# A two-layer backbone in split fp32: seven products in place of eight for 18 of the 22 gate/up blocks of the first feed-forward

## The reference, cut to what matters

```python
D_MODEL, SEQ, CTX_LEN = 1024, 512, 256
FFN_HIDDEN = -(-8 * D_MODEL // (3 * 256)) * 256    # 2816
def swiglu(h, w_in, w_out):
    gate, up = jnp.split(h @ w_in, 2, axis=-1)
    return (jax.nn.silu(gate) * up) @ w_out
...
x = x + gate_mod * swiglu(h, ffn_w_in[l], ffn_w_out[l])
```

## Time and profile before

| | |
|---|---|
| three runs, us | 2163.4, 2169.88, 2166.18 (median 2166.18) |
| the profiled execution, its own time | 2165.76 us, span 2164.0 us |
| mean granted TensorE clock | 0.986 of full speed |
| PE busy | 2087.6 us (96%) |
| DVE, ACT, POOL busy | 1083.9 us (50%), 821.9 us (38%), 67.6 us (3%) |
| layer 0's feed-forward, seen in the trace | about 627 to 1194 us |
| layer 1's feed-forward | about 1780 to 2140 us |

### The profile page before, as it was taken

The page is one execution under the profiler, slowest core; times in us unless marked ns, Lnnn a source line. Parts: engine busy times, 40 slices in busy tenths (PEclk is TensorE's granted clock), DMA queues, the critical chain, the costliest instruction groups (busy, mean ns, idle before and its releaser), DMA issues.

```text
span 2164.0 us, 33011 instructions
## 1 busy us (share of the span) xinstructions
PE 2087.6 (96%) x12961; PEld 1852.1 (86%) x12976; DVE 1083.9 (50%) x1577; ACT 821.9 (38%) x1265; POOL 67.6 (3%) x126
## 2 busy tenths in 40 slices
PE   6999999999999999999999999999998999999998
PEld 4899999998889999999999877777775788888887
...
DMA packets 297512, 204.42 MB, mean 94 GB/s; under 512 B 5012, under 2 KB 289037, under 8 KB 295629
## 3 DMA queue, kind: packets, MB, share of 16 engines
...
## 4 chain that ended last, share of the span: by engine, by line
PE 83%; DVE 7%; ACT 5%; issue 2%; DMA 1%; SPq 0%; ACTq 0%; POOL 0%; DVEq 0%; POOLq 0%
PE G L312 70%; ACT e L1461 1%; PE S L1599 1%; PE S L812 1%; DVE acc L1630 1%; PE S L1595 1%; PE S L783 1%; PE S L431 1%; DVE wlo L299 1%; DVE hn L684 1%; DMA adalo<-in_ada_w_dram 1%; DVE hlo L693 1%; ACT whi L295 1%; PE G L419 1%; PE S L807 1%
## 5 line engine op out<-in xcount | busy, mean ns | idle before, releaser
L312 PE MATMUL G<-hhi,whi 128*128 128x384 f32 (+2 forms) x2336 | 722.9, 367 | 28.0 <-DVE hlo L693 18.9
L312 PE MATMUL G<-hhi,wlo 128*128 128x384 f32 (+2 forms) x2336 | 679.0, 348 | 0.0
L312 PE MATMUL G<-hlo,whi 128*128 128x384 f32 (+2 forms) x2336 | 678.2, 348 | 0.0
L299 DVE TENSOR_TENSOR wlo<-raw,whi 128x1024 fp32r<-128x1024 f32 (+1 forms) x225 | 288.1, 1281 | 761.5 <-ACT whi L295 761.3
L295 ACT ACTIVATE whi<-raw 128x1024 fp32r<-128x1024 f32 (+1 forms) x225 | 249.3, 1108 | 953.5 <-PE G L312 604.6
L312 PEld LDWEIGHTS G<-hhi,whi 128*128 128x128 f32 x2336 | 422.5, 190 | 100.9 <-issue 46.7
L312 PEld LDWEIGHTS G<-hhi,wlo 128*128 128x128 f32 x2336 | 431.4, 190 | 20.0
L312 PEld LDWEIGHTS G<-hlo,whi 128*128 128x128 f32 x2336 | 431.9, 190 | 17.6
L312 PE MATMUL G<-mhi,whi 128*128 128x384 f32 (+2 forms) x550 | 165.7, 346 | 0.0
L312 PE MATMUL G<-mlo,whi 128*128 128x384 f32 (+2 forms) x550 | 165.3, 345 | 0.0
L312 PE MATMUL G<-mhi,wlo 128*128 128x384 f32 (+2 forms) x550 | 165.1, 345 | 0.0
...
## 6 DMA issues: line engine op xcount, KB each, us to landing
raw<-in_ffn_w_in_dram SPq DMA_DIRECT2D x88, 512.0 KB, 3.8
...
raw<-in_ssm_w_in_dram SPq DMA_DIRECT2D x41, 512.0 KB, 3.9
raw<-in_hg_w_in_dram SPq DMA_DIRECT2D x40, 512.0 KB, 3.9
adaw<-in_ada_w_dram SPq DMA_DIRECT2D x20, 1024.0 KB, 5.3
adaf<-in_ada_w_dram SPq DMA_DIRECT2D x20, 1024.0 KB, 5.3
raw<-in_ssm_w_out_dram SPq DMA_DIRECT2D x16, 512.0 KB, 4.1
...
```

The costliest lines, as they stand in the source:

```text
L299: dve.tensor_tensor(wlo[pn.slot][:, 0:kt, :], raw[pn.slot][:, 0:kt, :], f32(whi[pn.slot][:, 0:kt, :]), ALU.subtract).then_inc(s["lo"], 1)
L312: ins = pe.matmul(G[:, tl.slot, g0:g0 + n], w[pn.slot][:, k, :], r[:, k_base + k, t0:t0 + n], start=(first and k == 0 and i == 0), stop=(l ...
```

## The change

The gate and up panels of one hidden block are taken as one 2 x 2 block matrix: the two halves of the 1024 inputs by (gate, up). The activations are the other one: the same two input halves by the two token halves, named B11, B12, B21, B22. Eight products of half a panel (4 blocks) by 384 tokens make the block's result; Strassen's scheme makes it from seven, P1 to P7, of sums of the weights and sums of the activations. Each of the seven is 4 x 3 = 12 matmuls of 384 columns. `ON_TENSOR` is PE's order: P1, P6, P5, P7, P3, P2, P4. P2, P3 and P4 are added in PSUM onto the banks that hold P1, P5 and P7.

- The activation sums `T1`, `T2`, `T3` and `T4` are built once: ten VectorE instructions of 1536 elements (`combine`), four copies on ScalarE (`combined_hi`) and four subtractions on VectorE (`combined_lo`). They are spread over the first four blocks and over the down panels behind them.
- Per block the weight sums (P5, P6, P7, P3) are four VectorE instructions of 512 elements (`sum_weights`); seven half panels are split into hi and lo (`pair_hi`, `pair_lo`), one block ahead, into rings `shi`, `slo` of seven buffers. Five VectorE additions of 384 elements gather the results out of PSUM (`gather`); Silu, the multiplication by up, `mhi` and `mlo` are done per token half.
- The parts of layer 0's feed-forward are now 4, 6, 6, 6 blocks. The first four go as before, the other 18 by the new scheme. So there are 32 down panels (of 4 or 6 blocks) in place of 16 of 11. Layer 1's parts are 6, 8, 8 blocks, the matmuls as before, with 24 down panels in place of 16. Panel buffers hold 8 blocks in place of 11.
- Raw gate and up of a pair are loaded as two transfers of 512 KB into `sraw0` or `sraw1`; `sraw0` lies on `raw0` and `raw1`, and rings 0 to 3 on `whi` and `wlo`, so at the start and end of a part the buffers change hands.
- The modulation slabs stay 20: one after each of the first four gate panels, and 16 of them now in 16 of the 18 pairs, between P7 and P3. The zero matmuls that open and close a stack, the rows and the turn are moved with them.

```diff
-FH = FFN // P // 2
+PARTS = ((4, 6, 6, 6), (6, 8, 8))
+PK = KT
...
-            *[(f"raw{i}", (P, FH, P)) for i in (0, 1)],
-            *[(f"w{w}{i}", (P, FH, P), F32R) for i in (0, 1) for w in ("hi", "lo")],
+            *[(f"raw{i}", (P, PK, P)) for i in (0, 1)],
+            *[(f"w{w}{i}", (P, PK, P), F32R) for i in (0, 1) for w in ("hi", "lo")],
...
+        P1, P2, P3, P4, P5, P6, P7 = range(7)
+        RING = {P1: 0, P2: 1, P7: 2, P4: 3, P5: 4, P6: 5, P3: 6}
+        ON_TENSOR = (P1, P6, P5, P7, P3, P2, P4)
+        BANKS = {P1: 0, P2: 0, P6: 1, P5: 2, P3: 2, P7: 3, P4: 3}
+        SPLITS = ((P5, P6, P3, P1, P2, P7, P4), (P1, P5, P6, P7, P3, P2, P4))
+        SUMS = ((P5, P6, P3, P7), (P5, P6, P7, P3))
+        PAIRS = PARTS[0][1]
...
+        B11, B12, B21, B22 = quad(0, 0), quad(0, 1), quad(1, 0), quad(1, 1)
+        T4 = B12
+        MOVING = {P1: B11, P2: B21, P3: B22, P4: T4, P5: T1, P6: T2, P7: T3}
...
+            if first is not None and prod in (P1, P2, P7, P4):
+                eng.wait_ge(s["pan"], first.n + (KT - 1 if prod in (P1, P2) else KT))
+            elif U.past(1):
+                eng.wait_ge(s["spd"], ended(U + (-1), prod))
...
+        def sum_weights(dve, U, prod, first=None):
+
+            raw_in(dve, U)
+            ring_free(dve, U, prod, first)
+            if prod in (P6, P3):
+                dve.wait_ge(s["ssm"], sum_count(U, P5 if prod == P6 else P6, first))
+            a, b, op = {P5: (raw_quad(U, "up0"), raw_quad(U, P4), ALU.add),
+                        P6: (sum_of(P5), raw_quad(U, P1), ALU.subtract),
+                        P7: (raw_quad(U, P1), raw_quad(U, "up0"), ALU.subtract),
+                        P3: (raw_quad(U, P2), sum_of(P6), ALU.subtract)}[prod]
+            dve.tensor_tensor(sum_of(prod), a, b, op).then_inc(s["ssm"], 1)
+
+        def unsplit(U, prod):
...
+        def pair_hi(act, U, prod, first=None):
+            if prod in (P1, P2, P4):
+                raw_in(act, U)
+                ring_free(act, U, prod, first)
+            else:
+                act.wait_ge(s["ssm"], sum_count(U, prod, first))
+            act.activation(ring(prod)[0][:, :, :], unsplit(U, prod), ACT.Copy).then_inc(s["shi"], 1)
...
+        def pair_lo(dve, U, prod, first=None):
+            dve.wait_ge(s["shi"], split_count(U, prod, first))
+            hi, lo = ring(prod)
+            dve.tensor_tensor(lo[:, :, :], unsplit(U, prod), f32(hi[:, :, :]), ALU.subtract).then_inc(s["slo"], 1)
...
+        def pair_tensor(pe, U, first=None, between=None):
+            for prod in ON_TENSOR:
+                pe.wait_ge(s["slo"], split_count(U, prod, first))
+                if first is not None and prod in (P1, P5):
+                    last = first + (KT - 2 if prod == P1 else KT - 1)
+                    pe.wait_ge(took[last.slot], last.turn + 1)
+                elif first is None and prod == P1:
+                    pe.wait_ge(s["sg"], U.n * 2)
+                elif first is None and prod in (P5, P7):
+                    pe.wait_ge(s["sv"], U.n * 5 + (-1 if prod == P5 else 0))
+                if prod in (P2, P3, P4):
+                    pe.wait_ge(s["sv"], U.n * 5 + {P2: 1, P3: 2, P4: 3}[prod])
+                if first is not None and U.n == 0 and prod in (P6, P4):
+                    pe.wait_ge(s["tlo"], 3 if prod == P6 else 4)
+                opens = prod in (P1, P6, P5, P7)
+                hi, lo = ring(prod)
+                rhi, rlo = MOVING[prod]
+                for k in range(KH):
+                    for i, (w, r) in enumerate(((hi, rhi), (hi, rlo), (lo, rhi))):
+                        ins = pe.matmul(bank_of(prod), w[:, k, :], r[:, k, 0:EVEN],
+                                        start=(opens and k == 0 and i == 0),
+                                        stop=(k == KH - 1 and i == 2), skip_group_check=not opens)
+                ins.then_inc(s["spd"], 1)
+                if prod == P7 and between is not None:
+                    between()
+
+        def part_of(ap, j, th):
+            return ap[:, bass.ds(j, 1), th * EVEN:(th + 1) * EVEN].rearrange("p a t -> p (a t)")
...
+            if th:
+                act.wait_ge(s["sv"], U.n * 5 + 4)
+                act.activation(sx, sx, ACT.Silu).then_inc(s["sg"], 1)
+            else:
+                act.wait_ge(s["spd"], ended(U, P2))
+                if U.past(1):
+                    act.wait_ge(s["sml"], U.n * 2)
+                act.activation(sa, bank_of(P1), ACT.Silu).then_inc(s["sg"], 1)
+
+        def copy_first(act, U):
...
+            to, a, prod, own = ((sv, sv, P6, None), (sw, sv, P5, 1), (sw, sw, P7, 2), (sx, sv, P3, 1), (sv, sv, P4, 4))[n]
+            dve.wait_ge(s["spd"], ended(U, prod))
+            if own is None:
+                dve.wait_ge(s["sc"], U.n + 1)
+            else:
+                dve.wait_ge(s["sv"], U.n * 5 + own)
+            dve.tensor_tensor(to, a, bank_of(prod), ALU.add).then_inc(s["sv"], 1)
...
+        def mid_half(dve, U, th):
+            dve.wait_ge(s["sg"], U.n * 2 + (2 - th))
+            dve.wait_ge(s["sv"], U.n * 5 + (3 if th else 5))
+            dve.tensor_tensor(MIDS[th], MIDS[th], sw if th else sv, ALU.mult).then_inc(s["smid"], 1)
...
+        def pair_scalar(act, U, j, downs=None):
+            nxt = U + 1
+            if downs is None:
+                pair_hi(act, nxt, P1)
+            copy_first(act, U)
+            if downs is None:
+                for prod in (P5, P6, P7, P3):
+                    pair_hi(act, nxt, prod)
+            gate_half(act, U, 1)
+            gate_half(act, U, 0)
+            if downs is None:
+                pair_hi(act, nxt, P2)
+            mid_hi(act, U, j, 1)
+            if downs is None:
+                pair_hi(act, nxt, P4)
+            else:
+                act.wait_ge(s["spd"], ended(U, P2))
+                split_hi(act, downs, PAIRS)
+            mid_hi(act, U, j, 0)
+            if downs is not None:
+                act.wait_ge(s["spd"], ended(U, P4))
+                split_hi(act, downs + 1, PAIRS)
+
+        def pair_vector(dve, U, j, downs=None):
+            nxt = U + 1
...
+        def pair_vector(dve, U, j, downs=None):
+            nxt = U + 1
+            ahead = downs is None
+            if ahead:
+                pair_lo(dve, nxt, P1)
+            gather(dve, U, 0)
+            gather(dve, U, 1)
+            if ahead:
+                sum_weights(dve, nxt, P5)
+                sum_weights(dve, nxt, P6)
+            gather(dve, U, 2)
+            if ahead:
+                sum_weights(dve, nxt, P7)
+                pair_lo(dve, nxt, P5)
+            gather(dve, U, 3)
+            if ahead:
+                sum_weights(dve, nxt, P3)
+                for prod in (P6, P7, P3):
+                    pair_lo(dve, nxt, prod)
+            mid_half(dve, U, 1)
+            if ahead:
+                pair_lo(dve, nxt, P2)
+            mid_lo(dve, U, j, 1)
+            if not ahead:
+                split_lo(dve, downs, PAIRS)
+            gather(dve, U, 4)
+            mid_half(dve, U, 0)
+            if ahead:
+                pair_lo(dve, nxt, P4)
+            mid_lo(dve, U, j, 0)
+            if not ahead:
+                split_lo(dve, downs + 1, PAIRS)
+
+        def first_scalar(act, U, first):
+            for prod in SPLITS[0]:
+                pair_hi(act, U, prod, first)
+
+        def first_vector(dve, U, first, add):
...
+        def first_vector(dve, U, first, add):
+
+            for prod in (P5, P6, P3):
+                sum_weights(dve, U, prod, first)
+            for prod in (P5, P6, P3):
+                pair_lo(dve, U, prod, first)
+            add(KT - 2)
+            for prod in (P1, P2):
+                pair_lo(dve, U, prod, first)
+            sum_weights(dve, U, P7, first)
+            add(KT - 1)
+            for prod in (P7, P4):
+                pair_lo(dve, U, prod, first)
+
...
+            to, a, b, op, own = ((t1, hi[12], hi[11], ALU.subtract, 0), (t1, t1, lo[12], ALU.add, 1),
+                                 (t1, t1, lo[11], ALU.subtract, 2),
+                                 (t3, hi[22], hi[12], ALU.subtract, 0), (t3, t3, lo[22], ALU.add, 4),
+                                 (t3, t3, lo[12], ALU.subtract, 5),
+                                 (t2, hi[22], t1, ALU.subtract, 3), (t2, t2, lo[22], ALU.add, 7),
+                                 (t4, hi[21], t2, ALU.subtract, 8), (t4, t4, lo[21], ALU.add, 9))[n]
...
+                        if U.slot:
+                            sp.wait_ge(s["lo"], before.n + KT)
+                        if U.past(1):
+                            sp.wait_ge(s["slo"], U.n * 7 + (-6))
+                        r = sraw[1 - U.slot]
+                        blk = j + blocks_before(0, p)
+                        for h, c in ((0, 0), (1, FFN)):
+                            sp.dma_start(r[:, h, :, :], cols_of(w_in, blk * P + c)).then_inc(s[f"sraw{1 - U.slot}"], 16)
+                        if peeled and j == 0:
...
```

(53 more changed lines are left out.)

461 lines of the change are left out of this document (336 added, 125 removed).

## The result

The change takes 2135.0 us in the median of four runs (2130.08 to 2137.63); the kernel before took 2165.84 in the four beside it. The ratio is 0.9853, with a 95% interval of 0.9828 to 0.9878: 30.8 us faster. The profiled execution took 2137.63 us, its span is 2135.9 us.

The account below looks back on a forecast made before the run. PE's matmul count was taken as the bound. Removed matmuls -37.4 us, seams +3.3, +1.5, +0.4, +0.5, layer ends +1.0 and +0.3 sum to -30.4, giving 2135.5 us; range 2130 to 2151.

Parts of the forecast that it names:

- What goes from PE: In the 18 pairs, 84 matmuls replace 96: 2.08 us less per pair, 37.4 us in all; 15.77 us per pair with slab.
- Does VectorE keep up?: In each pair VectorE was put at 10.8 to 13.2 us of work, under the pair's 15.77 and 14.56 us.
- The deadline of 1.2 us at the second Silu: In each pair both Silus end by 14.6 us, before the next P1 at 15.8, leaving 1.2 us.
- The seams: Where blocks, pairs and down panels meet, PE loses time covered before; for layer 0's feed-forward 5.2 us.
- P1 behind part 0: After part 0's last down panel, PE waits for P1's split: 1.5 us lost.
- the step from the classic block to the down panels: At part 0's down panels in layer 0, less cover for the `mlo` split: 0.4 us lost.
- Pair to down panels: At three part ends the first down panel's split comes after the pair's matmuls: 1.1 us each, 3.3 in all.
- End of layer 0: Fewer matmuls cover the norm chain at the layer's end: 1.0 us lost, between -1 and +5.2.
- End of layer 1: By the same measure as the end of layer 0: 0.3 us lost; layer 1's part of 6 adds 0.5.
- VectorE did not take over: Rival in the pairs: VectorE's 20 instructions set the pair at 16.8 us, total 2153.5 us; chance 0.08.
- the seams were cheaper and not dearer: Rival at seams and layer ends: buffers changing hands cost 16 us more, total 2151.5 us; chance 0.12.
- the weights were not late: Rival in the pairs: raw weights over 14.3 us after their order delay ScalarE's first copy; at 17.3 us, 2189.5; chance 0.02.

Follow-up runs that it names:

- act1: The change with one more copy of 512 elements on ScalarE between the two Silus of each pair: 2137.45 us in one execution.
- late0: The change with each pair's raw weights ordered only when all seven splits of the pair before are written: 2212.86 us.
- late2: The change with each pair's raw weights ordered when the fifth split of the pair before is written, not the first: 2137.65 us in one execution.
- seam1: The change with the last split of T4 moved behind the splits that P1 needs: 2134.38 us in one execution.
- dve10: The change with ten more unused additions of 512 elements on VectorE in each pair, behind the first gather: 2230.07 us.
- seams: The change with T4's last split behind P1's splits and the first down panel's split ahead of the second token half's mhi and mlo: 2134.03 us.
- l1split: The kernel before with only layer 1's feed-forward in parts of 6, 8, 8 in place of 11, 11: 2164.5 us in one execution, beside 2166.98.

## Why the prediction was right

The predicted 2135.5 us met 2135.0, with four executions spread over 7.5 us. By its own steps:

- **What goes from PE** (12 matmuls at 0.1733 us, 37.4 us in all) holds: 15.77 us per pair to the hundredth, and 35.3 to 36.9 us when the twelve are put back. The cycle table of the Trainium skill ("VectorE: DVE Perf Modes", section "The TRN2 errata"), by which they would be 35.1, does not fit these matmuls: they stand 0.173 us apart in the changed kernel too.
- **Does VectorE keep up?** 11.9 us busy per pair, inside 10.8 to 13.2; 1.8 us more were free. The deadline of 1.2 us at the second Silu stands: one more copy on ScalarE was free, and six were not, at the place named. ScalarE in order of time, that Silu in a pair of part 1:

```profile
787.02 0.49 ACT L1233 ACTIVATE sa<-G 128x384 f32<-128x384 f32 x1
```

It ends at 787.5. The next pair starts at 788.7: four times 15.77 behind the first one's 725.63, shown below. That is the 1.2 us.
- **The seams.** P1 behind part 0 was put at 1.5. TensorE there:

```profile
723.55 0.34 PE L327 MATMUL G<-mhi,wlo 128*128 128x384 f32 x1
725.63 0.44 PE L1211 MATMUL G<-hhi,shi 128*128 128x384 f32 x1 [1.75 <-DVE slo L1187]
```

From start to start that is 2.08 us where matmuls stand 0.17 apart without a wait, so 1.9 are lost. In the same measure the step from the classic block to the down panels (692.79 to 693.45) costs 0.5 of 0.4 and layer 1's part of 6 some 0.7 of 0.5. *Pair to down panels*, put at 1.1 us three times, was too dear. Its own working gives 16.7 - 15.8 = 0.9, and not 1.1; and at the ends of parts 1 and 3 PE has the zero matmuls that close a stack to run just there. TensorE at the end of part 1:

```profile
820.18 0.34 PE L1211 MATMUL G<-hhi,slo 128*128 128x384 f32 x1
820.45 0.67 PE L470 MATMUL S<-ident,nil 128*32 128x128 f32 x16
821.20 0.58 PE L327 MATMUL G<-mhi,whi 128*128 128x384 f32 x2
```

and at the end of part 2:

```profile
966.07 0.34 PE L1211 MATMUL G<-hhi,slo 128*128 128x384 f32 x1
967.10 0.59 PE L327 MATMUL G<-mhi,whi 128*128 128x384 f32 x2 [0.69 <-issue]
```

At part 1 the zero matmuls (L470) fill the time up to 821.1: 1.02 us from start to start, where the kernel before has 0.86 around the same sixteen (802.10 to 802.96), so PE loses some 0.2 us. Part 3 shows the same 1.02. Part 2 has nothing there and loses 0.85 (1.03 us between two starts that are 0.17 apart without a wait). So the three places cost some 1.2 us and not 3.3; the working counted the zero matmuls as work and did not use them as cover. The five seams of layer 0 together cost 1.9 + 0.5 + 1.2 = 3.6 us of the 5.2 put down, which fits act1's stretch: 28.4 less against 27.0.
- **End of layer 0**, put at 1.0 with -1 to +5.2: the stretch behind the mark fell by 2.3 us in this profile, where 5.2 us of matmuls had gone, so the loss is 2.9. The other nine runs built on the change have the same code there, and in their profiles the loss goes from 0.1 (late0, late2) to 3.6 us (seam1). The stretch in the kernel before, the change, dve10 and late0, in the columns of the earlier trace rows:

```profile
1183.72:1401.43 217.71, 204.78 (x1048) 176.45 (x1051) 158.97 (x224) 128.12 (x235) 8.43 (x23) 0.96 0.20 59
1157.53:1372.98 215.45, 201.97 (x1018) 172.24 (x1021) 159.46 (x224) 128.42 (x235) 10.48 (x24) 0.95 0.21 59
1252.39:1466.48 214.09, 199.82 (x1018) 170.95 (x1021) 159.04 (x224) 128.22 (x235) 9.24 (x24) 0.96 0.21 60
1234.75:1447.30 212.55, 197.49 (x1022) 168.10 (x1021) 159.53 (x224) 128.14 (x235) 9.07 (x23) 0.98 0.21 60
```

The clock goes with most of it: 0.95 in the six runs that lose 1.3 to 3.6 us, 0.97 and 0.98 in the two that lose 0.1. dve10 and seams stand at 0.96 like the kernel before and lose 1.6 and 1.7; so at the same granted clock the shorter cover costs some 1.6 us, an estimate from two profiles, and the 1.0 was 0.6 too low. Where the lower clock falls then adds or takes up to 2 us from one execution to the next. Why it falls in different places in the same code stays open.
- **End of layer 1**, for 0.8 with the part of 6: 1.0 + 0.4 in l1split, 1.0 - 0.7 in the change. The last piece is 10.5 us in five profiles of the change and its variants and 11.5 to 11.8 in the other five, with 11.2 before, so 0.3 to 1.6 is what the profiles show.

So the mechanism holds: the matmuls that are gone are worth their distance, the other engines stay covered, and the rest is lost at seams and ends. The two misses, seams 1.6 us too dear and the end of layer 0 too cheap, by 0.6 at the same clock and by 1.9 in this profile, are of opposite sign; that the median came within 0.5 us is luck, as one execution differs from the next by more. The rivals did not come: VectorE did not take over, the seams were cheaper and not dearer, and the weights were not late. The point at which the last one was said to decide was wrong, though: 14.3 us from the order to ScalarE's first copy. late2 left 3.4 of these 14.3 us and the pair stayed at 15.77, because the copy only holds up the gather that P3 waits for, and by the prediction's own times P3 starts at 9.5, some 7 us behind the 2.1 at which ScalarE wants the weights.
